# Score products of a gated recurrence on TensorE: blocks of up to 128 keys, or pairs of 32 keys and 32 queries in four column tiles

## What is computed

```python
b = jnp.cumsum(log_f, axis=3)
q_dec   = q * jnp.exp(b)
k_intra = k * jnp.exp(-b)
scores  = jnp.einsum('bhncd,bhnsd->bhncs', q_dec, k_intra)
scores  = jnp.where(tri_mask, scores, 0.0)
o_intra = jnp.einsum('bhncs,bhnse->bhnce', scores, v)
# and from chunk to chunk: o_c = q_c . state; state = decay * state + k_c v_c
```

## Time and profile before

| | before |
|---|---|
| median of 3 runs | 1770.09 us |
| the profiled execution's own time | 1770.73 us |
| its span, first to last instruction | 1769.0 us |
| TensorE busy with matmuls | 1664.5 us, 94% |
| TensorE weight loads | 871.4 us, 49% |
| VectorE, ScalarE, GpSimd | 30%, 23%, 9% |
| mean granted TensorE clock | 0.967 |
| line 1502 in the chain that ended last | 4% |

### The profile page before, as it was taken

The page is one execution under the profiler, slowest core; times in us unless marked ns, Lnnn a source line. Parts: engine busy times, 40 slices in busy tenths (PEclk is TensorE's granted clock), DMA queues, the critical chain, the costliest instruction groups (busy, mean ns, idle before and its releaser), DMA issues.

```text
span 1769.0 us, 16715 instructions
## 1 busy us (share of the span) xinstructions
PE 1664.5 (94%) x5606; PEld 871.4 (49%) x5606; DVE 533.8 (30%) x1103; ACT 400.6 (23%) x604; POOL 164.4 (9%) x213
## 2 busy tenths in 40 slices
PE   6999999999999998999985999999999999999990
PEld 4444445656555554555564444444444444444440
DVE  4441044535426444434447011111111111111114
ACT  6011043454345333212430000000000000000003
POOL 1001000000000000000002011111111111111100
PEclk9999999999999998999985999999999999999995
DMA  7222131232131314434654899999999999999957
GB/s 232 90 84 77 66 131 60 66 102 101 49 110 68 124 38 144 153 128 164 250 202 144 310 336 334 335 334 336 333 336 333 334 335 334 333 335 333 335 186 297
DMA packets 171211, 371.24 MB, mean 210 GB/s; under 512 B 8992, under 2 KB 46368, under 8 KB 171040
## 3 DMA queue, kind: packets, MB, share of 16 engines
q1 hardware_dynamic: 152160, 304.62, 48.9%
q0 software_dynamic: 18720, 65.02, 12.1%
q10 hardware_dynamic: 288, 1.05, 0.1%
HBM read 304.60 MB, written 66.06 MB: 210 GB/s over the span
## 4 chain that ended last, share of the span: by engine, by line
PE 92%; DVE 3%; ACT 2%; DMA 2%; issue 1%; DVEq 0%; SPq 0%; POOLq 0%; ACTq 0%
PE bank L1423 28%; PE bank L1675 27%; PE bank L1699 13%; PE bank L1548 6%; PE bank L1502 4%; PE bank L1590 2%; PE bank L1668 2%; PE bank L1507 1%; PE bank L1524 1%; PE bank L1523 1%; PE bank L1609 1%; PE bank L1690 1%; PE bank L1486 1%; PE bank L1643 1%; PE bank L1453 1%
## 5 line engine op out<-in xcount | busy, mean ns | idle before, releaser
L1423 PE MATMUL bank<-wide,mid 128*128 128x512 f32 x1152 | 499.9, 593 | 0.8 <-DVE wide L971 0.8
L1675 PE MATMUL bank<-wup,xgT 128*128 128x512 f32 x1088 | 480.4, 594 | 1.4 <-ACT xgT L926 1.4
L1423 PEld LDWEIGHTS bank<-wide,mid 128*128 128x128 f32 x1152 | 218.2, 191 | 269.9 <-issue 268.4
L1675 PEld LDWEIGHTS bank<-wup,xgT 128*128 128x128 f32 x1088 | 204.7, 191 | 246.3 <-issue 244.2
L1699 PE MATMUL bank<-wide,hidT 128*128 128x512 f32 x544 | 240.8, 596 | 4.2 <-DVE hidT L1384 4.2
L1699 PEld LDWEIGHTS bank<-wide,hidT 128*128 128x128 f32 x544 | 101.4, 191 | 119.2 <-issue 119.2
L1548 PE MATMUL bank<-early,mid 128*128 128x512 f32 x288 | 125.7, 596 | 0.0
L933 ACT ACTIVATE sil<-bank 128x512 f32<-128x512 f32 x34 | 20.3, 597 | 434.8 <-PE bank L1675 434.8
L1357 DVE TENSOR_SCALAR mid<-bank,gate_of 128x512 f32<-128x512 f32 x68 | 51.1, 751 | 212.2 <-PE bank L1699 212.2
L723 POOL DMA_INDIRECT x_dram<-mid,sidx x34 | 53.6, 1577 | 644.0 <-DVE mid L1357 297.3
L926 ACT ACTIVATE xgT<-bank 128x512 f32<-128x512 f32 x70 | 38.1, 595 | 277.4 <-PE bank L1668 277.4
(11 more groups left out here) (198 smaller groups left out, 1344.6 us busy)
## 6 DMA issues: line engine op xcount, KB each, us to landing
wup<-w SPq DMA_DIRECT2D x68, 2048.0 KB, 17.8
wide<-w SPq DMA_DIRECT2D x34, 2048.0 KB, 10.2
u_dram<-ustage POOLq DMA_DIRECT2D x60, 256.0 KB, 2.3
rin<-u_dram SPq DMA_DIRECT2D x60, 256.0 KB, 3.7
mid<-w_in SPq DMA_DIRECT2D x24, 512.0 KB, 3.8
early<-x_all SPq DMA_DIRECT2D x12, 512.0 KB, 3.4
mix_dram<-mixst POOLq DMA_DIRECT2D x24, 256.0 KB, 2.7
mid<-x_all SPq DMA_DIRECT2D x12, 512.0 KB, 5.4
```

Of the source, the lines that this page charges most:

```text
L1423: last = pe.matmul(PROJ[u % 3][:, :], wsec[:, slot, k, :], nT[:, k, g * GT:(g + 1) * GT], start=(k == 0), stop=(k == KT - 1))
L1675: last = pe.matmul(bank[out_bank][:, :], xgT[:, k, :], weights[:, s, k, :], start=(k == 0), stop=(k == KT - 1))
```

## The change

`key_span` and the sorted loop go. A score product is now made for each pair of a sub-block of 32 keys (`i`) and a sub-block of 32 queries (`j`) that counts: ten pairs for a chunk, so 40 matmuls in a step instead of 16, each with 32 columns of weights and 32 streamed columns over all 128 channels. Each writes the 32 PSUM partitions of its keys and stands in the column tile of these partitions (`tile_position=(0, k0)`). The loops run over the distance `away` between the sub-blocks, then over the chunks `b`, then over the key sub-blocks `i`, so that consecutive matmuls mostly have different column tiles. Semaphores, other engines and all other lines stay as they are.

```diff
-            def key_span(d, j):
-
-                keys = SUB * (j + 1 if d == FWD else NSUB - j)
-                return keys if keys <= P // 2 else P
-
             def scores_and_updates(h, n):
                 d, g = STEPS[n]
                 r = h * NS + n
                 ge(pe, st_ready, r)
-                for keys, j in sorted((key_span(d, j), j) for j in range(NSUB)):
-                    lo, hi = (0, keys) if d == FWD else (P - keys, P)
+                for away in range(NSUB):
                     for b in range(BG):
-                        c0 = b * P + j * SUB
-                        last = pe.matmul(SC[lo:hi, c0:c0 + SUB], lev[d][:, b, j * P + lo:j * P + hi],
-                                         qs[:, c0:c0 + SUB], start=True, stop=True)
+                        for i in range(NSUB):
+                            j = i + away if d == FWD else i - away
+                            if not 0 <= j < NSUB:
+                                continue
+                            c0, k0 = b * P + j * SUB, i * SUB
+                            last = pe.matmul(SC[k0:k0 + SUB, c0:c0 + SUB], lev[d][:, b, j * P + k0:j * P + k0 + SUB],
+                                             qs[:, c0:c0 + SUB], start=True, stop=True, tile_position=(0, k0))
                 last.then_inc(sc_ready, 1)
                 pe.wait_ge(ktok_ready, r + 1)
```

## The result

The changed kernel takes 1744.12 us (median of 4 runs, 1742.89 to 1748.72), the kernel before 1770.55 us beside it (1769.51 to 1774.43). The ratio is 0.9848, with a 95% interval of 0.9834 to 0.9862: 1.5% faster. My point, 1768, was 24 us off; the time lies in the stated range, on the rival "the tiles overlap", whose price was 1746.5. In the profiled execution (1748.72 us, the slowest of the four) the span is 1747.1 us against 1769.0.

A forecast was written before the change was run, and what follows sets the result against it. TensorE was taken to bound the recurrence; 2.1 us from 23 steps plus 0.5 us from the step at the lower clock made 2.6 us off 1770.73, stated as 1768 us, range 1741 to 1774.

The forecast's parts named there:

- the tiles overlap: Score products: at each of 852 tile changes the second tile's load is hidden, 0.0317 us each; 24 us, 1746.5; chance 0.32.
- What bounds the kernel: Recurrence: TensorE is busy 410.67 of 415.00 us, so what a step gives up at the scores comes off nearly whole.
- Instructions and changes of shape: Score products: 80 records cost 0.03 to 0.05 us more, one shape change fewer saves 0.12; 0.09 us less a step.
- (4): Score products: 852 changes of column tile between consecutive matmuls, taken to gain or cost zero.
- far end: Scores with further overlap: key copies hold all steps, backward about 1.3 us, four forward about 0.9; floor 1741.
- Step (5): Scores hide ScalarE's key copy, ending 2.12 us after their start in eight forward steps, 1.19 backward; at 2.67 us both stay hidden.
- Step (7): Instruction fetch: 1152 more loads and as many more matmul records, costed at nothing; fetching queues take 0.1% of DMA time.
- The slow rival: Score products: each of 852 tile changes costs 0.027 us, 23 us less 2.6, so 1791; chance 0.17.

## Why the prediction failed at its point and held in its range

**What bounds the kernel: right.** The scores' time came off the end except for the gap in the loop, the slow stretch at it, and a longer wait at line 1484, all counted below.

**Instructions and changes of shape: right.** With one tile at a time the scores take 2.34 us, and the last distance after the change runs at 0.0317 a record as I read it. That order gave 1764.2 where I had 1768; the difference, 24 x 0.33 = 8 us less and 2.8 + 2.7 us more for the gap in the loop and what follows it, is two things I had left out, of opposite sign; 1.3 us of it stay open.

**The column tiles: wrong.** The step that failed is (4): "I take zero, because the nearest rows say it: the pace is fully explained by loads that go one after another". The rows of before could not say it. All of them stand in one tile, and a pace bound by that tile's own loads looks the same as one bound by a single way on for all loads. I took the absence of a case for evidence about it. The right reading was that 0.0317 us is the pace of a tile, and four tiles give four times it. The Trainium skill's two sentences, weighed against each other there, are settled as well: "TensorE: Matmul & The Clock Gate", part 3, The mechanism, has tiles work side by side, and the trace agrees (0.008 us a record with four tiles). The same part, What overlaps and what doesn't, lets a load overlap a running matmul only between different row groups; here the trace disagrees: all products use all rows, and within 0.26 us 33 loads have started beside 30 matmul records.

**The rival "the tiles overlap": right in kind, short in size.** I priced one of two records hidden, 1.54 us a step; the records of all tiles run fully side by side and it is 1.13 to 1.25. What I had as the far end, in which the key copies hold the steps, is nearly what came in nineteen steps (eight forward, eleven backward); the four first forward steps are held by their fullest tile, at 1.13 and not 0.9. Measured: eleven backward steps 2.76 to 1.25, four forward 2.76 to 1.13, eight forward 2.76 to 2.17, and the one at the lower clock 5.00 to 1.87. Together 16.6 + 6.5 + 4.7 + 3.1 = 31 us. The step at the lower clock gave 0.9 more behind its scores: from its first score to the next step's it is 31.07 us before and 27.04 after. Of these 31.9 us 24.7 are left in the middle stretch; 2.8 went into the gap, 2.7 into the clock after it, and 1.2 into a longer wait at line 1484 (9.3 against 8.1), which closes the account to within 0.5. So it is in part luck that the rival's 1746.5 stands 2.4 us from the 1744.1 measured: its 24 us were 7 short of what the scores gave up, and the three losses, 6.7 us together, were in no sum of mine.

**The cover: right, and it decided.** Step (5) named the wait for the key copy in eight forward steps at about 2.2 us if the scores became shorter than 2.1. It came at 2.17, in those eight steps, and giving it cover again brought 9.6 us. That the backward steps are held too, by 0.07 us each, follows from the copy's end at 1.19 us, which step (5) gives as well.

**Instruction fetch: wrong.** Step (7) costed it at nothing, "eight records at 0.031 us run without a gap". The records are not where it is late. It is late at the jump, where the kernel before had no fetch at all. I had looked at the share of the fetching queues over the run, not at when they fetch.

**The slow rival** had no sign: a change of tile costs nothing measurable.

## What to carry to other kernels

Small products with few output partitions are worth spreading over the column tiles, one product of each tile in turn or two: the order alone was worth 20 of 26 us here, and the fullest tile is then the least time they take. When a stretch of the bounding engine shrinks to less than half, list what it covered and when that ends, before asking what it gains; the next wait was readable to 0.1 us in the trace of before. And when a loop body grows, look at whether its second round fetches instructions and whether a gap stands at the jump back.

## What the runs showed of the hardware

Products of float32 with 32 columns of weights and 32 streamed run at 0.0317 us a record in one column tile, and at about 0.0105 and 0.008 a record in three and four tiles in turn, with all 128 rows in use. Each tile takes records as if from a queue of its own: beside the running record about three can wait, and the way on shuts while one such queue is full (next tile's start after 0.013, 0.09 and 0.15 us with two, three and four products in a row, the first a third of the 0.04 in which three more tiles started). So matmuls of different tiles do not start in the order of the program; those of one tile seem to. A step that ran at 1.2 GHz shortened too, from 5.00 to 1.87 us. And a gap of 2.8 us at a loop's jump, with one instruction packet fetched in it, brought 7 us at 1.2 GHz in the same execution, which by the estimate above nearly doubled its price.
